# Two changes on TensorE's queue in a two-layer trunk: matmuls ordered by token segment, and fourteen modulation units moved from TensorE to VectorE

## The reference, cut to what matters

```python
mod_x = einsum('bd,lde->lbe', silu(c), w_ada) + b_ada[:, None, :]      # w_ada: (2, 1024, 6144)
mod_c = einsum('d,lde->le', silu(c_ctx), w_ada) + b_ada
for i in range(2):
    sh1, sc1, g1, sh2, sc2, g2 = split(mod_x[i]); csh1, ..., cg2 = split(mod_c[i])
    hx = rmsnorm(x, norm_mix[i]) * (1 + sc1) + sh1                      # hc likewise from ctx
    ox, oc = gla_mixer(hx, hc, ...) if i == 0 else swa_mixer(hx, hc, ...)
    x = x + g1 * ox
    x = x + g2 * swiglu(rmsnorm(x, norm_ffn[i]) * (1 + sc2) + sh2, ffn_w_in[i], ffn_w_out[i])
    ...                                                                 # the same for ctx, in layer 0 only
return rmsnorm(x, norm_final)
```

## Time and profile before

| | |
|---|---|
| median of 3 runs | 1669.13 us (1669.12 to 1671.03) |
| the profiled execution's own time | 1669.12 us |
| its span, first to last instruction | 1667.4 us |
| mean granted TensorE clock | 0.989 of full speed |
| PE busy | 1618.1 us, 97% of the span |
| VectorE busy | 864.4 us, 52% |
| ScalarE busy | 577.4 us, 35% |
| POOL busy | 99.2 us, 6% |
| DMA | 156.07 MB, mean 94 GB/s |

### The profile page before, as it was taken

How to read it: one execution, slowest core, us unless ns; L and a number is a source line. 1 busy time by engine, 2 the same in 40 slices (tenths; PEclk the granted TensorE clock), 3 DMA queues, 4 the chain that set the end, 5 groups by cost and what they waited for, 6 DMA issues and landing times.

```text
span 1667.4 us, 24130 instructions
## 1 busy us (share of the span) xinstructions
PE 1618.1 (97%) x9568; PEld 1370.2 (82%) x9568; DVE 864.4 (52%) x1426; ACT 577.4 (35%) x833; POOL 99.2 (6%) x96
## 2 busy tenths in 40 slices
PE   7999999999999999999999999979999999999998
PEld 5889988888888888888888888757778788888886
DVE  5314436644576566556566336678755533333334
ACT  4315447542432111122102124457744422222223
POOL 0000000000000000000000000036540000000003
PEclk8999999999999999999999999979999999999999
DMA  9341310013443433343343213320003232333332
GB/s 335 100 128 54 106 44 26 26 51 102 127 127 101 125 127 112 115 126 102 125 126 103 74 57 108 101 76 2 1 1 101 76 101 87 90 100 101 101 88 88
DMA packets 197310, 156.07 MB, mean 94 GB/s; under 512 B 6691, under 2 KB 194255, under 8 KB 197231
## 3 DMA queue, kind: packets, MB, share of 16 engines
q1 hardware_dynamic: 197230, 154.97, 30.4%
HBM read 149.71 MB, written 2.10 MB: 91 GB/s over the span
## 4 chain that ended last, share of the span: by engine, by line
PE 88%; DVE 4%; ACT 4%; issue 1%; SPq 1%; DMA 1%; DVEq 0%; ACTq 0%
PE ps L577 85%; PE ps L1110 1%; ACT w_hi L1189 1%; DVE w_lo L1667 1%; DMA ada_pre<-in_w_ada 1%; PE ps L1115 1%; SPq L376 1%; DVE q_st L2192 1%; DVE h_lo L1730 1%; DVE scaled L1721 0%; ACT h_hi L1239 0%; ACT pr L1624 0%; DMA q_sw<-q_rot 0%; PE ps L892 0%; SPq L495 0%
## 5 line engine op out<-in xcount | busy, mean ns | idle before, releaser
L577 PE MATMUL ps<-h_hi,w_hi 128*128 128x256 f32 (+1 forms) x1392 | 422.3, 362 | 6.9 <-DVE w_lo L1667 6.8
L577 PE MATMUL ps<-h_hi,w_lo 128*128 128x256 f32 (+1 forms) x1392 | 413.6, 355 | 0.0
L577 PE MATMUL ps<-h_lo,w_hi 128*128 128x256 f32 (+1 forms) x1392 | 410.1, 353 | 0.0
L1667 DVE TENSOR_TENSOR w_lo<-w_raw,w_hi 128x2048 fp32r<-128x2048 f32 (+1 forms) x88 | 197.2, 2240 | 219.1 <-ACT w_hi L1189 218.9
L577 PEld LDWEIGHTS ps<-h_hi,w_hi 128*128 128x128 f32 x1392 | 257.3, 190 | 51.9 <-issue 13.5
L1189 ACT ACTIVATE w_hi<-w_raw 128x2048 fp32r<-128x2048 f32 (+1 forms) x88 | 165.1, 1876 | 386.0 <-DMA w_raw<-in_ffn_w_in 207.3
L577 PEld LDWEIGHTS ps<-h_lo,w_hi 128*128 128x128 f32 x1392 | 263.7, 189 | 38.3
L577 PEld LDWEIGHTS ps<-h_hi,w_lo 128*128 128x128 f32 x1392 | 262.9, 189 | 37.0
L577 PE MATMUL ps<-a_hi,w_hi 128*128 128x512 f32 (+1 forms) x528 | 160.5, 359 | 0.0
L577 PE MATMUL ps<-a_hi,w_lo 128*128 128x512 f32 (+1 forms) x528 | 160.1, 358 | 0.0
L577 PE MATMUL ps<-a_lo,w_hi 128*128 128x512 f32 (+1 forms) x528 | 158.0, 354 | 0.0
(11 more groups left out here) (246 smaller groups left out, 2011.7 us busy)
## 6 DMA issues: line engine op xcount, KB each, us to landing
w_raw<-in_ffn_w_in SPq DMA_DIRECT2D x88, 512.0 KB, 4.9
ada_w<-in_w_ada SPq DMA_DIRECT2D x41, 1024.0 KB, 5.3
w_raw<-in_ffn_w_out SPq DMA_DIRECT2D x32, 512.0 KB, 4.4
w_raw<-in_gla_w_in SPq DMA_DIRECT2D x24, 512.0 KB, 4.9
ada_pre<-in_w_ada SPq DMA_DIRECT2D x7, 1024.0 KB, 11.8
w_raw<-in_ffn_w_out SPq DMA_DIRECT2D x16, 384.0 KB, 3.5
w_raw<-in_gla_w_o SPq DMA_DIRECT2D x8, 512.0 KB, 7.2
w_raw<-in_swa_w_o SPq DMA_DIRECT2D x8, 512.0 KB, 5.0
```

The lines of the kernel that those rows point to most:

```text
L577: return pe.matmul(o, w, r, start=start, stop=stop, skip_group_check=skip)
L1667: dve.tensor_tensor(w_lo[s][:, 0:kc, :], raw_of(n)[:, 0:kc, :], w_hi[s][:, 0:kc, :].bitcast(F32), ALU.subtract).then_inc(wlo_ok, 1)
```

## The change

Three things are edited together.

1. In every slab with both segments (and in the gates' narrow slab), the loop over segments is moved outside those over chunks and products, and runs LAT first: six 512-column matmuls, then six 256-column ones.
2. All 40 units are accumulated by VectorE. The two units of slabs 16 and 17 move on to the FFN's later slabs, up to 45. `unit` and `unit_turn` are gone. The sum over the partitions is now made for 512 values at once: ScalarE rounds `u_acc` to `u_hi` (`unit_high`), VectorE takes the rest `u_lo` (`unit_low`), TensorE multiplies both by a 128x128 block of ones (`unit_sum`, two single-pass matmuls of 512 columns into bank 7), and VectorE picks each column's own value out by a product with the identity, a reduction over 128 and the bias (`store_sum`). TensorE waits for `unit_low` before `unit_sum`, and in three places for `store_sum` (through `mod_ok`).
3. V's results are copied out of PSUM by ScalarE, behind the decays, and no longer by VectorE.

SyncE's queue is changed in two places: unit 1 is loaded ahead of slab 3, and the first FFN part's loop is cut into single pairs.

```diff
@@ slab (TensorE)
                     if k == 2 and turns is not None:
-                        unit_turn(turns, 2 * i)
+                        unit_sum(turns)
...
-                    for ch in chunks:
-                        blk = slice(ch * P, (ch + 1) * P)
-                        for j, (w, r) in enumerate(((w_hi, x_hi), (w_hi, x_lo), (w_lo, x_hi))):
-                            for sg in segs:
+                    for sg in reversed(segs):
+                        for ch in chunks:
+                            blk = slice(ch * P, (ch + 1) * P)
+                            for j, (w, r) in enumerate(((w_hi, x_hi), (w_hi, x_lo), (w_lo, x_hi))):
@@ units (TensorE)
-        def unit(a, i=0):
-            pe.wait_ge(mod_ok, a + 1 + i)
-            pe.wait_ge(in_unit, 16 * (a + 1) + i * 16)
-            for k in range(DC):
-                g = 32 * (k % 4)
-                last = mm(ps[g:g + 32, 6 * 512:6 * 512 + 256], c_pre[:, k, :], ada_w[:, k, :], k < 4, k >= 4)
-            last.then_inc(ada_done, 1)
         def unit_sum(a, i=0):
             pe.wait_ge(mod_ok, a + 1 + i)
-            pe.wait_ge(ada_done, a + 1 + i)
-            for e in range(2):
-                for m in range(2):
-                    last = mm(bank(6, 2 * e + m, 1), u_acc[:, m, e * P:(e + 1) * P], ones[:, 0:1], True, True)
+            pe.wait_ge(ul_ok, a + 1 + i)
+            for j, u in enumerate((u_hi, u_lo)):
+                last = mm(bank(7), ones_r[u_set(a)][:, :], u[u_set(a)][:, :, :].rearrange("p m n -> p (m n)"), j == 0, j == 1)
             last.then_inc(turned, 1)
@@ GO (TensorE)
             slab(n, 0, go_in, BOTH, before={...}, turns=unit_of(n) - 1 if n > GO0 else None)
-            unit(unit_of(n))
@@ first_slab (TensorE)
                 if k == 2 and turn is not None:
-                    unit_turn(turn)
+                    unit_sum(turn)
                 if k == 3:
                     if turn is not None:
                         pe.wait_ge(mod_ok, turn + 2)
@@ V (ScalarE)
             gate_log(h, d)
+            unit_high(n)
             decays(h, d)
-            unit_row(n)
+            act.wait_ge(slab_done, n + 1)
+            for j in range(3):
+                last = act.activation(gla_v[:, n - V0, 6 + 2 * j:8 + 2 * j, :].rearrange("p t n -> p (t n)"),
+                                      bank(slab_banks(n) + j), ACT.Copy)
+            last.then_inc(out_free[n % 2], 1)
@@ units (ScalarE, VectorE)
+        def unit_high(a, i=0):
+            act.wait_ge(ada_done, a + 1 + i)
+            act.wait_ge(turned, a + 1 + i)
+            ...
+            act.activation(u_hi[u_set(a)][:, :, :], u_acc[u_set(a)][:, :, :], ACT.Copy).then_inc(row_ok, 1)
+        def unit_low(a, i=0):
+            dve.wait_ge(row_ok, a + 1 + i)
+            dve.tensor_tensor(u_lo[u_set(a)][:, :, :], u_acc[u_set(a)][:, :, :], u_hi[u_set(a)][:, :, :].bitcast(F32),
+                              ALU.subtract).then_inc(ul_ok, 1)
-        def store_unit(a, i=0):
+        def store_sum(a, i=0):
             dve.wait_ge(turned, a + 2 + i)
+            part = u_acc[u_set(a)][:, :, :].rearrange("p m (e n) -> p (m e) n", n=P)
+            dve.tensor_tensor(part, bank(7).rearrange("p (c n) -> p c n", n=P),
+                              ident[:, :].rearrange("p (o n) -> p o n", o=1).to_broadcast([P, 4, P]), ALU.mult)\
+               .then_inc(up_ok, 1)
+            dve.wait_ge(up_ok, 2 * a + 1 + i * 2)
+            dve.tensor_reduce(den[:, :], part, AX.X, ALU.add).then_inc(up_ok, 1)
+            dve.wait_ge(up_ok, 2 * a + 2 + i * 2)
@@ GO (VectorE)
         for n in range(GO0, F0):
             split(n + 1)
+            unit_acc(unit_of(n))
+            unit_low(unit_of(n))
             plain(n, "gla", 2 * (n - GO0), 16, BOTH, False)
             raw_low(0, 2 * (n - GO0), BOTH)
-            store_unit(unit_of(n))
+            store_sum(unit_of(n))
             if n == F0 - 1:
-                dve.wait_ge(mod_ok, unit_of(F0) + 1)
+                dve.wait_ge(mod_ok, U1 + 1)
                 shifts(0, 24)
             raw_low(0, 2 * (n - GO0) + 1, BOTH)
```

More of the change, by code:

```diff
@@ L152, in trunk @@
     m_prev, m_next = m_both[:, 0:P], m_both[:, P:2 * P]
-    u_acc = at("u_acc", TM + 37504, [P, 2, 256])
+    u_acc = [at(f"u_acc{j}", TM + o, [P, 2, 256]) for j, o in enumerate((32768, 37504))]
+    u_lo = [at(f"u_lo{j}", TM + o, [P, 2, 256], F32R) for j, o in enumerate((32768, 37504))]
+    u_hi = [at(f"u_hi{j}", TM + o, [P, 2, 256], F32R) for j, o in enumerate((8 * ROW, 33408))]
+    ones_r = [at(f"ones_r{j}", TM + o, [P, P], F32R) for j, o in enumerate((34816, 35456))]
     scaled_t = [at(f"scaled{j}", TM + (7 + j) * ROW, [P, T]) for j in range(2)]
@@ L465, in ffn @@
                 j0 = 0
-                for pairs in ((2, 2), (4,), (2, 1))[PARTS.index((f0, fc))]:
+                for pairs in ((1, 1, 1, 1), (4,), (2, 1))[PARTS.index((f0, fc))]:
                     m = n + 2 * j0
@@ L796, in first_slab @@
                     last.then_inc(bw_done, 1)
-                    if turn is not None:
-                        unit(turn + 1)
                 pe.wait_ge(rl_ok, 8 * e + k + 1)
-                for ch in range(2):
-                    blk = slice(ch * P, (ch + 1) * P)
-                    for j, (w, r) in enumerate(((w_hi, raw_hi), (w_hi, raw_lo), (w_lo, raw_hi))):
-                        for sg in segs:
+                for sg in reversed(segs):
+                    for ch in range(2):
+                        blk = slice(ch * P, (ch + 1) * P)
+                        for j, (w, r) in enumerate(((w_hi, raw_hi), (w_hi, raw_lo), (w_lo, raw_hi))):
                             last = mm(seg(b0, ch, sg), w[s][:, k, blk], r(e, k, sg), start=(k == 0 and j == 0 and
@@ L816, in _ @@
         BOTH = (CTX, LAT)
[L817 to L821 removed]
+        pe.wait_ge(or_ok, 1)
+        slab(QK0 + 2, 0, h_in, BOTH, before={1: lambda: unit_sum(0), 7: lambda: unit_sum(1)})
+        slab(QK0 + 3, 0, h_in, BOTH, before={6: lambda: unit_sum(2)})
         pe.wait_ge(gwl_ok, 1)
[L825 removed]
+        pe.wait_ge(mod_ok, V0)
         for k in range(DC):
[L827 to L828 removed]
+            for sg in reversed(BOTH):
+                for j, (w, r) in enumerate(((g_whi, h_hi), (g_whi, h_lo), (g_wlo, h_hi))):
                     last = mm(S67[:, sg[0]:sg[1]], w[:, k, :], r[:, k, sg[0]:sg[1]], k == 0 and j == 0,
@@ L844, in _ @@
             for t in range(TILES):
-                if t == 1:
-                    if n == V0:
-                        pe.wait_ge(gl_ok, 1)
-                    unit_turn(n - 1)
-                if t == 2:
+                if t == 1 and n > V0:
+                    pe.wait_ge(za_ok, n - V0)
+                    unit_sum(n - 1)
+                if t == 2 and n == V0:
+                    pe.wait_ge(gl_ok, 1)
+                    unit_sum(n - 1)
+                if t == 2 + int(n == V0):
                     pe.wait_ge(mod_ok, n + 1)
@@ L953, in _ @@
             if h == 0:
-                unit_turn(R0 - 1)
+                pe.wait_ge(za_ok, 4)
+                unit_sum(R0 - 1)
             if ahead:
@@ L1015, in ffn @@
                 if lead:
-                    first_slab(n, 2 * l, segs, turn=unit_of(n) - 1 if has_unit(n) else None)
-                    a = unit_of(F0)
-                    slab(n + 1, 0, h_in, segs, k_wait=h_wait(2 * l + 1, per),
-                         before={1: lambda: unit_turn(a), 4: lambda: unit(a + 1), 7: lambda: unit_turn(a + 1)}
-                         if has_unit(n) else {})
+                    first_slab(n, 2 * l, segs, turn=U1 - 1 if l == 0 else None)
+                    slab(n + 1, 0, h_in, segs, k_wait=h_wait(2 * l + 1, per))
                 m = n + 2 * lead
@@ L1880, in _ @@
         dve.memset(g_w[:, :, :], 0.0).then_inc(gw_ok, 1)
+        dve.tensor_copy(ones_r[0][:, :], ones[:, :]).then_inc(or_ok, 1)
+        unit_acc(0)
         split(QK0 + 2)
-        store_unit(0)
+        unit_low(0)
+        store_sum(0)
+        unit_acc(1)
         split(QK0 + 3)
-        store_unit(1)
-        store_unit(2)
+        unit_low(1)
+        store_sum(1)
+        unit_acc(2)
         split(QK0 + 4)
+        unit_low(2)
         dve.wait_ge(gwh_ok, 1)
@@ L1889, in _ @@
            .then_inc(gwl_ok, 1)
-        store_unit(3)
+        store_sum(2)
+        unit_acc(3)
+        unit_low(3)
         def logs(h, d):
@@ L1934, in _ @@
         for n in range(V0, V0 + 4):
+            store_sum(n - 1)
             split(n + 1)
-            h, b0 = n - V0, slab_banks(n)
+            h = n - V0
+            unit_acc(n)
             logs(h // 2, h % 2)
+            unit_low(n)
             weights(h // 2, h % 2)
-            dve.wait_ge(slab_done, n + 1)
-            for j in range(3):
-                last = dve.tensor_copy(gla_v[:, h, 6 + 2 * j:8 + 2 * j, :].rearrange("p t n -> p (t n)"), bank(b0 + j))
-            last.then_inc(out_free[n % 2], 1)
-            store_unit(n)
+        store_sum(R0 - 1)
         def masks(h):
@@ L2089, in up @@
```

(3 more changed lines are left out.)

105 lines of the change are left out of this document (51 added, 54 removed).

## The result

| | before | after |
|---|---|---|
| median of 4 runs each, one chip | 1670.08 us (1669.12 to 1673.90) | 1658.76 us (1658.33 to 1659.28) |
| ratio, with its 95% interval | | 0.9928 (0.9911 to 0.9945) |
| repeated on another chip, beside the last experiments | 1672.93 us | 1658.52 us, 0.9917 (0.9903 to 0.9930) |
| span of the profiled execution | 1667.4 us | 1657.6 us |
| mean granted TensorE clock | 0.989 | 0.985 |

A forecast was written before the change was run, and what follows sets the result against it. TensorE was taken to bound the kernel. Gains of 16.9 + 11.4 + 9.9 + 1.1 = 39.3 us less waits of 2 + 8.8 + 4.8 = 15.6 left 23.7 us, so 1645.4 us, range 1631 to 1659.

The forecast's parts named there:

- Fourteen units less: TensorE: fourteen `unit` and `unit_turn` at 1.66 us give way to two 512-column matmuls at 0.45 us, 16.9 us gained.
- Twenty-six sums: TensorE: twenty-six one-column `ones,u_acc` sums of 0.89 us become new sums of 0.45 us, 11.4 us gained.
- The pitch of a pair: Slabs 18 to 49: 256- and 512-column pairs fall from 0.3533 to 0.3467 us through new order and sum, 9.9 us gained.
- Waits for `u_lo` in GO: GO: loads of `ada_w` come 20.0 us apart, so TensorE waits for the units, 8.8 us lost.
- Slab 16's third step: Slab 16: TensorE waits ahead of the statistics until unit 11 is stored, 4.8 us lost.
- V: V: VectorE's added work fits slabs of 19.3 us; bank 2 us late for R's scores at V's end, 2 us lost.
- QK's wait for `u_row`: QK: TensorE's wait for a `u_row` ahead of the gates' slab goes, 1.1 us gained.
- VectorE in FFN0: FFN0: `unit_low` behind the split leaves `u_lo` ready with 1.3 us to spare, so no wait.
- the pitch stays: Rival: pairs stay at 0.353 us, so 9.9 us are missing and the time is 1655.3 us; chance 13%.

The follow-up runs named there:

- the last experiments: Changed kernel with SyncE's GO queue turned round, unit 11's wait one step later, and alternating 512-first order: mixed with grouped 1646.36 us, in every slab with both segments 1647.78 us.
- the identity matmul: Changed kernel with the old order, plus one fp32 128x128 matmul with identity weights behind the unit sum in every even slab from 18: 1661.64 us, one run.

## Why the prediction was right in direction and half wrong in size

- **Fourteen units less, 16.9 us; new sum at 0.45.** Right. The sum is 0.46 us (494.91 to 495.37), and in V, where no pair's pace plays in, four units less won 4.4 us beside the new wait of 1.2, 1.1 a unit for the 1.21 of the forecast.
- **Twenty-six sums, 11.4 us.** Right within 0.3 (0.89 for 0.46).
- **The pitch of a pair, 9.9 us. This is the step that failed**, in its cause first. The prediction took "TensorE is thrown into a slower pattern by the one-column fp32 matmuls" from one jump and concluded that order and sum "should end that". The runs show that the new sum does not end it (17.42 us a slab with the old order), and that the grouped order has a third pace, 0.350. FFN0 won 1,488 x 0.0033 = 4.9 us, half; the order alone shows nearly the same (540.3 to 535.1 us from slab 18's sum on). That in QK, R and GO "the order brings nothing" was wrong too: 0.3467 became 0.350 in QK and 0.350 to 0.353 in GO, some 1.6 us lost over their pairs. What the rows of before did allow was one step more of doubt: the jump at 491.50 came behind the first `ones,u_acc`, but also behind the last `ada_w,c_pre`, and that wide fp32 matmuls restore the fast pace, as the identity matmul does, explains the same rows. Two things had changed there, and I named one. Neither is the whole cause, as the pairs of QK show that run at either pace behind the same matmuls.
- **Waits for `u_lo` in GO, 8.8 us.** Mechanism right (the queue; turned round, they go), size 5.4. SyncE's queue of the changed kernel shows the loads of three units:

```profile
375.33 0.37 SPq L414 DMA_DIRECT2D ada_w<-in_w_ada  x1
...
395.33 0.37 SPq L414 DMA_DIRECT2D ada_w<-in_w_ada  x1
...
413.97 0.37 SPq L414 DMA_DIRECT2D ada_w<-in_w_ada  x1
```

  They are 20.0 us apart, as forecast, and then 18.6: the forecast took the first period for all. The chain that ended last has the piece that differs, the load of a slab (start us, us, what):

```profile
376.37 8.60 DMA w_raw<-in_gla_w_o
...
396.37 7.25 DMA w_raw<-in_gla_w_o
```

- **Slab 16's third step, 4.8 us.** Measured 4.36, right. **What it sets off was missing**: 3.9 us at the low clock, a term put at nothing without a reason, though the old trace had two such stalls with the low clock behind them (1087.69 and 1106.92). This is the second step that failed, and it almost doubles the stall. With the idle time filled the clock stays at 1.00 and slabs 16 to 18 are 4.2 us shorter.
- **V.** Slab 19.4 us for 19.3, wait at its end 1.2 for 2. Right. **QK's wait for `u_row`** is gone, right.
- **VectorE in FFN0.** No wait for `u_lo` in any loop slab, right. One wait of 1.1 us for `w_lo` ahead of slab 18 was not forecast.
- **Not in the sum at all:** 1.2 us at the start, ahead of the first slab, while TensorE waits for the load of a unit (0.7 to 1.3 us in all runs with the new units, none in the one without them; cause not found), and 1.8 us given back in layer 2. Its cause is open. TensorE waits longer for the softmax there (9.6 us in four waits for 7.8), but the repetition waits 4.6 us for the first softmax, where the changed kernel's first profile has 6.9 and before 4.8, and layer 2 is no shorter in it (637.7 us for 637.4). Counted from layer 2's first statistics, only 0.6 us of the 1.8 are lost up to the first softmax's scores, and another 1.0 between the attention and FFN1's statistics.

Of the rivals, "the pitch stays" with 1655.3 us was the nearest, in part by luck: half of the pitch's gain came, and the low clock, the start and layer 2 took more than that away again. Its rule has no gain from any order: the Trainium skill ("TensorE: Matmul & The Clock Gate", Back-to-back issue gap) gives one gap by the columns, columns / 2.4 + 2.5 ns, and calls it that of a single matmul; its other figure, about 131 ns for 512 columns in a stream with weight loads, no row here shows (226). Neither its one price nor my two are right: at full clock the rows show 0.3467, 0.350 and 0.3533 us for the same pair. At the low clock the same section's columns / 1.2, 427 and 213 ns, is exactly what slab 16 shows (445.18 to 445.60, 447.52 to 447.74).
